# Two transformer stacks on one core: the mixing layers' first two projections as one 512-column pair, and a new order of their events

## What is computed

```python
h = rms_norm(x, attn_norm[l])
proj = h @ w_in[l]
qa, ka, va, qb, kb, vb, qc, kc, vc, cq, ckv, kr = jnp.split(proj, split_points, axis=-1)
o_a = neighborhood_attention(qa, ka, va, na_rpb[l])            # 4 heads of 64
o_b = diff_attention(qb, kb, vb, lam, lam_init, ...)           # 4 heads, two softmaxes, a norm after
o_c = dilated_attention(qc, kc, vc, t5_dil)                    # 4 heads
cq = rms_norm(cq, mla_q_norm[l]);  ckv = rms_norm(ckv, mla_kv_norm[l])
o_d = mla_attention(...)                                       # 4 heads, from cq (256), ckv (128), kr (32)
x = x + jnp.concatenate([o_a, o_b, o_c, o_d], axis=-1) @ w_o[l]
h = rms_norm(x, ffn_norm[l])
x = x + (jax.nn.silu(h @ w_gate[l]) * (h @ w_up[l])) @ w_down[l]
```

## Time and profile before

| | us |
|---|---|
| median of 3 runs | 1156.51 |
| lowest, highest | 1156.18, 1157.13 |
| the profiled execution | 1156.47 |
| its span, first to last instruction | 1154.5 |
| TensorE busy | 1130.9 |
| VectorE busy | 778.6 |
| ScalarE busy | 536.2 |
| mean granted TensorE clock | 0.996 |

### The profile page before, as it was taken

How to read it: one execution, slowest core, us unless ns; L and a number is a source line. 1 busy time by engine, 2 the same in 40 slices (tenths; PEclk the granted TensorE clock), 3 DMA queues, 4 the chain that set the end, 5 groups by cost and what they waited for, 6 DMA issues and landing times. The chain is left out here.

```text
span 1154.5 us, 17146 instructions
## 1 busy us (share of the span) xinstructions
PE 1130.9 (98%) x6716; PEld 986.8 (85%) x6716; DVE 778.6 (67%) x998; ACT 536.2 (46%) x704; POOL 32.9 (3%) x47
## 2 busy tenths in 40 slices
PE   6999999999999999999999999999999999999997
PEld 5888888898888888879988888888899888888886
DVE  5766666846667666677576676666766766766665
ACT  5533433556654334444566443334446655343332
POOL 0000000000000000003000000000030000000000
PEclk9999999999999999999999999999999999999999
DMA  8765566664346555668423465556773234656550
GB/s 266 242 208 187 183 212 197 204 219 130 127 149 229 188 182 182 207 153 263 146 103 102 150 227 197 182 182 200 180 235 110 75 111 145 219 188 203 180 193 37
DMA packets 167132, 204.59 MB, mean 177 GB/s; under 512 B 19988, under 2 KB 150028, under 8 KB 167078
## 3 DMA queue, kind: packets, MB, share of 16 engines
q1 hardware_dynamic: 167078, 203.84, 55.0%
HBM read 202.66 MB, written 1.16 MB: 177 GB/s over the span
## 5 line engine op out<-in xcount | busy, mean ns | idle before, releaser
L633 ACT ACTIVATE whi<-raw 128x2048 fp32r<-128x2048 f32 x176 | 336.5, 1914 | 382.5 <-PE bank L1511 245.5
L945 DVE TENSOR_TENSOR wlo<-raw,whi 128x2048 fp32r<-128x2048 f32 x171 | 392.2, 2294 | 165.8 <-ACT whi L633 165.8
L1507 PE MATMUL bank<-h_both,whi 128*128 128x512 f32 x1280 | 304.6, 390 | 0.0
L1507 PEld LDWEIGHTS bank<-h_both,whi 128*128 128x128 f32 x1280 | 237.7, 188 | 47.7
L1481 PE MATMUL bank<-whi,o_hi 128*128 128x512 f32 x448 | 176.2, 393 | 0.6 <-DVE o_lo L1253 0.6
L1482 PE MATMUL bank<-wlo,o_hi 128*128 128x512 f32 x448 | 174.9, 390 | 0.0
L1483 PE MATMUL bank<-whi,o_lo 128*128 128x512 f32 x448 | 174.4, 389 | 0.0
L1511 PEld LDWEIGHTS bank<-h_both,wlo 128*128 128x128 f32 x1280 | 164.1, 191 | 6.2
L1511 PE MATMUL bank<-h_both,wlo 128*128 128x256 f32 x1280 | 166.0, 283 | 0.0
L1481 PEld LDWEIGHTS bank<-whi,o_hi 128*128 128x128 f32 x448 | 84.3, 188 | 18.3 <-issue 2.3
L1483 PEld LDWEIGHTS bank<-whi,o_lo 128*128 128x128 f32 x448 | 84.1, 188 | 18.0
(11 more groups left out here) (175 smaller groups left out, 1202.3 us busy)
## 6 DMA issues: line engine op xcount, KB each, us to landing
raw<-in_w_gate_up SPq DMA_DIRECT2D x44, 1024.0 KB, 5.1
raw<-in_w_down SPq DMA_DIRECT2D x44, 1024.0 KB, 4.9
raw<-in_w_gate SPq DMA_DIRECT2D x22, 1024.0 KB, 5.4
raw<-in_w_up SPq DMA_DIRECT2D x22, 1024.0 KB, 5.3
raw<-in_w_in SPq DMA_DIRECT2D x20, 1024.0 KB, 6.4
raw<-in_w_o SPq DMA_DIRECT2D x12, 1024.0 KB, 5.0
raw<-in_w_kv SPq DMA_DIRECT2D x8, 1024.0 KB, 5.6
raw<-in_w_q SPq DMA_DIRECT2D x4, 1024.0 KB, 5.4
```

What stands on the lines that cost most here:

```text
L633: act.activation(whi[:, s, :], raw[:, s, :], ACT.Copy).then_inc(hi_ready, 1)
L945: dve.tensor_tensor(wlo[:, s, :], raw[:, s, :], whi[:, s, :].bitcast(F32), ALU.subtract).then_inc(lo_ready, 1)
L1507: pe.matmul(bank[bk + jj][:, :], hi[:, kc, jj * P:(jj + 1) * P], h_both[:, kc, :, :].rearrange("p a t -> p (a t)"), start=(kc == 0), stop= ...
```

## The change

Units are renumbered: 0 is cq, 1 is va, 2 is ckv and kr, 3 is ka, 4 is qa, and 5 to 14 are as before. Units 0 and 1 run as one pair, token tile by token tile, with the body that the later feed-forward stages had (now `first_pair`), into bank 4 (tile 0) and bank 5 (tile 1), 256 columns each for cq and va. Whole matmuls are of 512 columns except tile 0's products with the low weights. The head runs earlier on ScalarE and in another order on VectorE; every later gap between attention steps gets the next unit; unit 12 is issued in two halves, by token tile; unit 11 waits for the differential group's norm before its second tile only. In the first mixing layer ScalarE's copies of h come before two squares, and VectorE's scaled rows after the low copies. The diff, without the renumbered sources and bank numbers and without the feed-forward stage's call of the shared function:

```diff
-    s += unit(0) + unit(1) + unit(2) + [("mla_T",)] + unit(3) + [("mla_B",), ("mla_G",)] + unit(4)
-    s += S(0, 1) + N(0, 1) + unit(5)
-    s += TH(0, 1) + S(2, 3) + N(2, 3) + unit(6)
-    s += TH(2, 3) + S(4, 5) + N(4, 5) + V(0, 1, 2, 3) + [("O", 0)] + S(6, 7) + N(6, 7) + unit(7)
-    s += TH(4, 5) + S(8, 9) + N(8, 9) + TH(6, 7) + V(4, 5) + S(10, 11) + N(10, 11) + unit(8)
-    s += TH(8, 9) + S(12, 13) + N(12, 13) + V(6, 7) + [("O", 1)] + V(8, 9) + S(14, 15) + N(14, 15) + unit(9)
-    s += TH(10, 11) + V(10, 11) + [("diff_stats",)] + S(16, 17) + N(16, 17) + [("diff_norm",)] + unit(10)
-    s += [("diff_T",)] + S(18, 19) + N(18, 19) + TH(12) + unit(11)
-    s += TH(13, 14) + V(12, 13) + TH(15) + unit(12)
+    s += [("pair",), ("split", 2), ("proj", 0), ("proj", 1), ("split", 3)]
+    s += [("unit", 2), ("split", 4), ("proj", 2)] + unit(3) + [("mla_T",)] + unit(4) + [("mla_B",), ("mla_G",)] + unit(5)
+    s += S(0, 1) + N(0, 1) + unit(6)
+    s += TH(0, 1) + S(2, 3) + N(2, 3) + [("unit", 7), ("split", 9)]
+    s += TH(2, 3) + S(4, 5) + N(4, 5) + V(0, 1, 2, 3) + [("O", 0), ("proj", 7)] + S(6, 7) + N(6, 7) + unit(8)
+    s += TH(4, 5) + S(8, 9) + N(8, 9) + TH(6, 7) + V(4, 5) + S(10, 11) + N(10, 11) + unit(9)
+    s += TH(8, 9) + S(12, 13) + N(12, 13) + V(6, 7) + [("O", 1)] + V(8, 9) + S(14, 15) + N(14, 15) + unit(10)
+    s += TH(10, 11) + V(10, 11) + [("diff_stats",)] + S(16, 17) + N(16, 17) + [("diff_norm",)] + unit(11)
+    s += [("diff_T",)] + S(18, 19) + N(18, 19) + TH(12) + [("tile", 12, 0), ("split", 14)]
+    s += TH(13, 14) + V(12, 13) + TH(15) + [("tile", 12, 1)]
...
-        W_IN_COLS = [2304, 2560, 256, 0, 512, 1024, 768, 1280, 1792, 1536, 2048]
+        W_IN_COLS = [2304, 512, 2560, 256, 0, 1024, 768, 1280, 1792, 1536, 2048]
...
@@ -836,10 +837,10 @@
                         square_x(0, h)
                         square_scaled(0, h)
                     split(u0 + 1)
+                    h_out(6, 0, 0)
+                    h_out(6, 0, 1)
                     square_x(1, 0)
                     square_x(1, 1)
-                    h_out(6, 0, 0)
-                    h_out(6, 0, 1)
                     square_scaled(1, 0)
                     square_scaled(1, 1)
                     for h in range(2):
...
                         elif n == 1:
-                            act.wait_ge(units_used, u0 + 2)
+                            for t in range(TT):
+                                i = act.activation(vg[:, 1, t, :], bank[4 + t][:, cols[1]], ACT.Copy)
+                            i.then_inc(proj_out, 1)
...
@@ -1027,6 +1035,7 @@
                 mean_square(7, 1)
                 normalise(8, 1, 0)
                 normalise(8, 1, 1)
+                split(MIX_U[1] + 1)
                 h_lo_out(8, 1, 0)
                 h_lo_out(8, 1, 1)
 
...
@@ -1357,15 +1366,14 @@
                 for h in range(2):
                     h_lo_out(6, 0, h)
                 mean_squares(1)
-                residual_out(0, 0)
                 for h in range(2):
                     mixer_input(1, h)
-                residual_out(0, 1)
+                split(MIX_U[0] + 1)
                 for h in range(2):
                     h_lo_out(6, 1, h)
-                split(MIX_U[0] + 1)
-                for h in range(2):
-                    residual_out(1, h)
+                for t in range(TT):
+                    for h in range(2):
+                        residual_out(t, h)
 
             def mix(l):
                 i0, q0, p0 = stage_items(l)
...
@@ -1547,15 +1554,33 @@
                     mm = pe.matmul(dst, h[:, kc, tile(t)], w[:, kc, :], start=(first and kc == 0), stop=(last and kc == KC - 1))
                 return mm
 
-            def tile_hi(n, dst, t, j):
-
-                hi, lo = w8(n)
+            def pair_pass(n, bk, t, h, w, j=None, first=False, last=False):
+
+                for kc in range(KC):
+                    if first and kc % 4 == 0:
+                        pe.wait_ge(hT_hi, 4 * HT_NO[j] + 2 * t + kc // 4 + 1)
+                    mm = pe.matmul(bank[bk][:, :], h[:, kc, tile(t)], pair_of(w, n, kc),
+                                   start=(first and kc == 0), stop=(last and kc == KC - 1))
+                return mm
+
+            def first_pair(n, bks, j, tile0_done):
+
+                cols = pair_cols(n)
+                pe.wait_ge(hi_ready, n + 2)
+                pair_pass(n, bks[0], 0, h_hi, whi, j, first=True)
+                wait_h(j, 0)
+                pair_pass(n, bks[0], 0, h_lo, whi)
                 pe.wait_ge(lo_ready, n + 1)
-                for kc in range(KC):
-                    if kc % 4 == 0:
-                        pe.wait_ge(hT_hi, 4 * HT_NO[j] + 2 * t + kc // 4 + 1)
-                    pe.matmul(dst, h_hi[:, kc, tile(t)], hi[:, kc, :], start=(kc == 0), stop=False)
-                    pe.matmul(dst, h_hi[:, kc, tile(t)], lo[:, kc, :], start=False, stop=False)
+                tile_pass(bank[bks[0]][:, cols[0]], 0, h_hi, w8(n)[1], kcs=range(0, 4))
+                transposes(j, 1, (0,))
+                tile_pass(bank[bks[0]][:, cols[0]], 0, h_hi, w8(n)[1], kcs=range(4, KC))
+                transposes(j, 1, (1,))
+                pair_pass(n, bks[1], 1, h_hi, whi, j, first=True)
+                pe.wait_ge(lo_ready, n + 2)
+                tile_pass(bank[bks[0]][:, cols[1]], 0, h_hi, w8(n + 1)[1], last=True).then_inc(tile0_done, 1)
+                wait_h(j, 1)
+                pair_pass(n, bks[1], 1, h_lo, whi)
+                pair_pass(n, bks[1], 1, h_hi, wlo, last=True).then_inc(units_used, 2)
 
             def last_two_by_tile(n, chunks, ready, j):
 
...
@@ -1855,15 +1859,27 @@
                 t_of = {}
                 for ev in mix_script():
                     k = ev[0]
-                    if k == "unit":
+                    if k == "pair":
+                        first_pair(u0, (4, 5), j, mix_tile0)
+                    elif k == "tile":
+                        n, t = ev[1:]
+                        if t == 0:
+                            pe.wait_ge(lo_ready, u0 + n + 1)
+                            pe.wait_ge(out_lo, OUT_LO[l][1] + 1)
+                        mm = residual(u0 + n, MIX_OUT_CHUNK[n - 11], O, False, False, (t,))
+                        if t:
+                            used(mm)
+                    elif k == "unit":
...
                             used(mm)
-                        elif n < 13:
-                            if n == 11:
-                                pe.wait_ge(proj_out, p0 + 9)
-                                pe.wait_ge(d_n, l + 1)
-                                pe.wait_ge(out_lo, OUT_LO[l][1] + 1)
-                            else:
-                                pe.wait_ge(out_lo, OUT_LO[l][1] + 1)
-                            mm = residual(u, MIX_OUT_CHUNK[n - 11], O, n == 11, False)
-                            used(mm)
+                        elif n == 11:
+                            pe.wait_ge(proj_out, p0 + 9)
+                            pe.wait_ge(out_lo, OUT_LO[l][0] + 1)
+                            residual(u, MIX_OUT_CHUNK[0], O, True, False, (0,))
+                            pe.wait_ge(d_n, l + 1)
+                            pe.wait_ge(out_lo, OUT_LO[l][1] + 1)
+                            used(residual(u, MIX_OUT_CHUNK[0], O, True, False, (1,)))
                         elif n == 14:
                             last_two_by_tile(u - 1, MIX_OUT_CHUNK[2:4], [OUT_LO[l][i] + 1 for i in (2, 3)], 7 + 2 * l)
                     elif k == "mla_T":
```

More of the change, by code:

```diff
@@ L1658, in ffn @@
                     transposes(j, 0)
-                gate = [bank[ACC[t]][:, gate_up_cols(f)[0]] for t in range(TT)]
-                up = [bank[ACC[t]][:, gate_up_cols(f)[1]] for t in range(TT)]
-                gate_lo, up_lo = w8(u0)[1], w8(u0 + 1)[1]
-                def pair_pass(t, h, w, first=False, last=False):
-                    for kc in range(KC):
-                        if first and kc % 4 == 0:
-                            pe.wait_ge(hT_hi, 4 * HT_NO[j] + 2 * t + kc // 4 + 1)
-                        mm = pe.matmul(bank[ACC[t]][:, :], h[:, kc, tile(t)], gate_up_pair(w, f, kc),
-                                       start=(first and kc == 0), stop=(last and kc == KC - 1))
-                    return mm
@@ L1680, in ffn @@
                     pe.wait_ge(lo_ready, u0 + 1)
[L1681 removed]
+                    tile_pass(bank[banks_[0]][:, pair_cols(u0)[0]], 0, h_hi, w8(u0)[1])
                     wait_h(j, 1)
[L1683 removed]
+                    pair_pass(u0, banks_[1], 1, h_lo, whi)
                     pe.wait_ge(lo_ready, u0 + 2)
[L1685 to L1696 removed]
@@ L1875, in mix @@
                             used(mm)
-                        elif n == 0:
-                            first_token_major(u, bk, 0, j)
-                            transposes(j, 1)
-                            used(first_token_major(u, bk, 1, j))
-                        elif n < 11 and (n - 2) % 3 == 2:
+                        elif n in (7, 10):
```

78 lines of the change are left out of this document (37 added, 41 removed).

## The result

| kernel | median, us | runs | lowest to highest |
|---|---|---|---|
| before | 1156.18 | 7 | 1155.74 to 1157.13 |
| after | 1161.34 | 7 | 1160.07 to 1163.57 |

A forecast was written before the change was run, and what follows sets the result against it. It took TensorE, 98% busy, as the bound. Twice 3.53 us lost in the tails, 1.80 and 1.54 gained in the heads, give +3.7: 1156.47 + 3.7 = 1160.2 us, range of 0.8 from 1157.4 to 1163.6.

The forecast's parts named there:

- the tails: End of each mixing layer: 21.54 us instead of 23.85 with one 5.84 unit less, loss 3.53 us a layer.
- Head of the second layer: Second mixing layer's start: latent queries and va as a pair take 11.94 us instead of 13.74, gain 1.80.
- Head of the first layer: First mixing layer's start: 1.8 us wait for low copies, kr waits 1.0 us, gain 1.54 us.
- ScalarE's copies ahead of the squares: First mixing head: TensorE starts at 517.2, then a new 1.8 us wait takes the old one's place.
- First new wait: Each tail, between unit 11's tiles: tile 1 waits for VectorE's norm (d_n), 2.1 us.
- Second new wait: Each tail, within V(12), V(13): TensorE waits for ScalarE's copy of transposed rows behind the long copy, 1.4 us.
- Half units: Each tail: unit 12 cut in two tiles, a half priced at 2.78 us, the whole at 5.55.
- near 1 outside the first head: Expected sign: granted clock near 1 except at the first mixing head; a fall at 935 would prove it wrong.
- the clock falls after the new wait: Rival, tails: clock falls after the waits, up to 1.7 us a layer; 1161.5 to 1163.7; chance 0.22.
- the first wait doesn't arise: Rival, tails: the norm is done in time or the wait binds later, 4.2 us go; 1156.0; chance 0.12.
- both waits are absent: Rival, tails: only fewer, wider matmuls count, no new waits; 1153.2 us; chance 0.05.
- the heads give nothing: Rival, heads: kr or ka waits in the second layer too, up to 3.3 us lost; 1162 to 1163.5; chance 0.08.

The follow-up runs named there:

- e9: The kernel with the norm and the long copy moved, every 512-column matmul of all six pairs written as two of 256; 1155.44 us.
- e4: The changed kernel with ScalarE's old order at the first mixing head, two squares ahead of the first two copies of transposed rows; 1164.15 us.
- r2: The same edit as e4 to the changed kernel, measured again beside the changed kernel itself; 1162.07 us.
- e1: The changed kernel with the group's norm moved on VectorE ahead of the two softmax scalings; 1156.95 us.
- e6: The changed kernel with 9 useless matmuls of 512 columns between unit 11's tiles in each mixing layer, filling the wait; 1160.71 us.
- e8: The changed kernel with the bank-7 half of unit 11's second tile ahead of the wait for the norm; 1157.39 us.
- e2: The changed kernel with ScalarE's long copy of unit 14's high weights behind the copies of heads 13 and 14; 1158.32 us.
- r1: The changed kernel measured once more, with no edit; 1161.82 us.
- e3: The changed kernel with the norm ahead of the softmax scalings and the long copy behind the copies of heads 13 and 14; 1153.43 us.
- e5: The kernel before with only ScalarE's order at the first mixing head changed, two copies of transposed rows ahead of two squares; 1156.47 us.
- e7: The changed kernel with norm and long copy moved, and unit 11's tile 1 bank-7 half ahead of the wait; 1153.35 us.

## Why the prediction was right, and where it was not

It said 1160.2 us; the medians are 1161.34 and 1161.82. Its sum describes a run of after in which no clock falls, and those took 1159.5 to 1160.4. Taken from the profiles, that sum is 1156.47 + 2 x (21.93 - 18.01) - 1.80 - 2.24 = 1160.3. That this comes within 0.1 us of the forecast is luck: the tails lose 0.78 us more than I said (7.84 against 7.06), the heads gain 0.70 more (4.04 against 3.34), and the two errors cancel. The two waits, their places and their releasers are not luck. Step by step:

- **Head of the second layer**, gain 1.80: 1.80. But its reason was only partly the matmuls. I wrote that 80 replaced pairs are 1.3 us by the rows. e9 gives 0.48 us in the second head and nothing in the first. The other 1.3 us of the second head are for the most part waits of before, ahead of the transposes (the last pass starts at 836.44 and has 0.96 us of work, the transposes start at 837.88) and behind them (1.44 us to the next matmul, for 0.7 us of work).
- **Head of the first layer**, gain 1.54: 2.24, the term that was most off. The new wait for the low copies came (1.63 us, said 1.8), but kr waited 0.30 instead of 1.0. I had added whole durations on VectorE, and neighbours in one queue overlap by about 0.1 us (a row at 528.54 of 1.41 us is followed by one at 529.86); it also came to va's low parts 0.46 us sooner, counted from the transposes (523.82 - 516.00 = 7.82 us against the sum's 524.07 - 515.79 = 8.28). The clock didn't fall here.
- **ScalarE's copies ahead of the squares**: I priced the new wait as taking the place of the old one, and e4 and r2 show just that.
- **First new wait**, 2.1 us a layer: unit 11 takes 7.76 to 7.80 where its work is 5.55, so 2.2. It ends on L1458 as forecast. e1, e6 and e8 show that it is the norm and the bank that tile 1 writes.
- **Second new wait**, 1.4: transposes and products of heads 12 to 15 take 4.29 instead of 2.70, so 1.6, the smaller part of it (0.3) at the transposes. e2 shows that ScalarE's long copy was its cause. The row itself says 0.55, as the ends of matmuls are modelled: 953.11 to 954.26 is what passed. The sum was 0.2 short, mainly because it took V(13) to begin at 944.83, where three of the eight output matmuls and 1.04 us to unit 12 were left; behind the wait four are left, and 954.26 to 955.68 takes 1.42. It also set the new end of ScalarE's copy (938.87) against the old start of VectorE's low part (937.21), a shift of 1.66 us where the transposes move by 1.83; the maxima came 0.25 us sooner behind the transposes (949.36 - 946.54 against 938.67 - 935.60) and hid that.
- **Half units** cost 0.12 a layer more than the whole one, which I had at nothing.
- **The clock** is where the text was wrong: "near 1 outside the first head". A fall in the tail was one of its own signs of being wrong, and it came, at 942 us in after and at 941 in r1. The rival that the clock falls after the new wait came true in five tails of ten, at 1.5 to 1.7 us each, as it was priced (up to 1.7). I had taken it as a case that comes or doesn't, with 0.22 for it; it comes in some tails and not in others of the same execution, and six of r1's seven runs have the time and the mean clock of one fall in a tail. That is the 1.1 to 1.6 us between the forecast and the medians. My reason against it, that dense matmuls stand on both sides, does not hold. The granted clock was also at half at 28 us in the profile of before, which I had overlooked.
- The rivals in which the first wait doesn't arise, and in which both waits are absent (1153.2), did not come; e3, which takes both away, took 1153.4. Nor did the one in which the heads give nothing: the second head ended without a wait.

On the price of the narrow matmul the page of the Trainium skill that the prediction weighed (TensorE: Matmul & The Clock Gate, section Back-to-back issue gap) gives 2.5 ns for the second matmul, from its price of an isolated one. e9 measures 12 ns, less than the rows I used (16) and more than the page.

## What to carry to other kernels

A merged or widened step saves little by itself; it also takes a unit of cover from a place elsewhere, so walk every in-order queue at the gaps that lose it, and move small late-needed results (a norm, a copy) ahead of long early ones first: here two moved rows turned 5 us lost into 3 us gained. An idle stretch of TensorE costs more than its length if the granted clock falls behind it in some executions; the spread of the runs with their mean clock is a sign of that, one profile is not enough, and only a profile says where the fall lies. A filler of useless work shows cleanly which part of a loss is the wait and which the clock.

## What the hardware did that I had not expected

**The fall of the clock is not sure.** Behind the same 1.89 us of waiting (2.1 between the last start of work and the next) it came in five cases of ten, and both ways within one execution (r1). Behind 2.07 us at the first head it came in the profile of before and in neither of e4 and r2; behind 1.6 us at that head in none of the profiles with the copies first. What decides between the cases is not shown. A fall at 28 us stands in seven of the fourteen profiles (before, after, e1, e3, e5, e8, e9) and costs too little to tell: the transposes of the first mixing head start at 515.1 to 516.0 us in these seven, and at 515.1 to 516.4 in the five others that did not start late.

**A slow start that the mean granted clock does not show.** Most kernels, the one before too (1160.03 us), have a few runs some 3.5 us longer with a mean clock of 0.999. The profiles of e6 and e7 are such runs. Window from 16 to 18 us, the kernel before:

```profile
16.00:18.00 2.00, 2.00 (x21) 2.00 (x20) 1.55 (x3) 1.84 (x3) 0.00 (x0) 1.00 1.03 370
```

and the same window of e6:

```profile
16.00:18.00 2.00, 2.00 (x11) 2.00 (x11) 0.69 (x1) 0.89 (x2) 0.00 (x0) 1.00 1.06 375
```

Both read a granted clock of 1.00, but e6 runs half as many matmuls in the same time. Neighbouring matmuls of its first projection start 0.21 us apart until 22.82 us, and 0.12 after that:

```profile
22.61 0.38 PE L1490 MATMUL bank<-whi,h_both 128*128 128x256 f32 x1
22.82 0.28 PE L1488 MATMUL bank<-whi,h_both 128*128 128x256 f32 x1
22.95 0.28 PE L1489 MATMUL bank<-wlo,h_both 128*128 128x256 f32 x1
```

At that moment stands the trace's first record of the granted clock, at full. It is at 22.82 us in e6, at 22.84 in e7, and at 13.2 to 16.1 in the twelve other traces. Ahead of its first record the view prints 1.00, and the run's mean counts that stretch as full, so the mean clock can't tell a late run from an undisturbed one. The spacing of the matmuls says that TensorE ran at half the rate there. The first feed-forward head begins at 30.3 us in e6 against 27.5 in r1, and all that follows is later by as much. Why the clock rises late in some executions is not shown. It is not tied to the change: the kernel before has such runs, and none of after's fourteen has. Anyone who compares medians of this kernel at the level of 0.3% should set such runs aside by their start.
